# Where one layer's modulations are computed, and into how many pieces two feed-forward layers cut their hidden activations

## The reference

```python
mod = split_cols((sc @ w_mod[l] + b_mod[l])[:, None, :], (D_MODEL,) * N_MOD)
mod_x = split_cols(sc_ctx @ w_mod[l] + b_mod[l], (D_MODEL,) * N_MOD)
...
x = layer_norm(ALPHA * x + g1 * y) * ln1_g[l] + ln1_b[l]
x = layer_norm(ALPHA * x + g2 * swiglu_2(modulate(x, sh2, sc2), w_ffn_in[l], w_ffn_out[l])) \
    * ln2_g[l] + ln2_b[l]
...
def swiglu_2(h, w_in, w_out):
    a, b = h @ w_in[:, :D_FF_2], h @ w_in[:, D_FF_2:]
    return (jax.nn.silu(a) * b) @ w_out
```

## Time and profile before

| | |
|---|---|
| median of 3 runs | 3349.62 us |
| lowest and highest | 3346.73 and 3352.74 us |
| span of the profiled execution | 3342.8 us |
| PE busy | 3245.9 us, 97% of the span |
| DVE busy | 1693.8 us, 51% |
| ACT busy | 1329.2 us, 40% |
| POOL busy | 474.2 us, 14% |
| matmuls | 24670 |

### The profile page before, as it was taken

How to read it: one execution, slowest core, us unless ns; L and a number is a source line. 1 busy time by engine, 2 the same in 40 slices (tenths; PEclk the granted TensorE clock), 3 DMA queues, 4 the chain that set the end, 5 groups by cost and what they waited for, 6 DMA issues and landing times. The chain is left out here.

```text
span 3342.8 us, 59968 instructions
## 1 busy us (share of the span) xinstructions
PE 3245.9 (97%) x24670; PEld 3027.7 (91%) x24686; DVE 1693.8 (51%) x2839; ACT 1329.2 (40%) x2350; POOL 474.2 (14%) x471
## 2 busy tenths in 40 slices
PE   8999999999999999999999999999999999999998
PEld 7999988887778999999789889999998889889997
DVE  4666643546634456665545773222227646743334
ACT  4222222346633432225348663112125547552224
POOL 1010010036400010011013201001010114110100
PEclk9999999999999999999999999999999999999999
DMA  4444422122122344453201421111223212422222
GB/s 162 161 171 171 144 83 70 59 77 60 55 82 95 101 141 169 171 176 110 66 20 42 133 91 64 58 63 58 64 65 125 92 50 54 148 71 95 89 92 92
DMA packets 94973, 325.23 MB, mean 97 GB/s; under 512 B 10800, under 2 KB 15152, under 8 KB 94576
## 3 DMA queue, kind: packets, MB, share of 16 engines
q1 hardware_dynamic: 90992, 307.19, 28.0%
q0 software_dynamic: 3280, 13.68, 1.2%
q10 hardware_dynamic: 432, 0.52, 0.0%
HBM read 309.96 MB, written 2.10 MB: 93 GB/s over the span
## 5 line engine op out<-in xcount | busy, mean ns | idle before, releaser
L2403 DVE TENSOR_TENSOR r_Wbasel<-r_Wf,r_Wbaseh 128x1024 fp32r<-128x1024 f32 (+1 forms) x298 | 380.0, 1277 | 536.3 <-ACT r_Wbaseh L1770 535.9
L1770 ACT ACTIVATE r_Wbaseh<-r_Wf 128x1024 fp32r<-128x1024 f32 (+1 forms) x298 | 307.9, 1037 | 438.8 <-PE PS L1139 340.1
L1137 PE MATMUL PS<-r_X1h,r_Wbaseh 128*128 128x264 f32 (+2 forms) x1216 | 391.0, 322 | 13.0 <-DVE r_X1l L2644 3.7
L1137 PE MATMUL PS<-r_X2h,r_Wbaseh 128*128 128x256 f32 (+1 forms) x1224 | 373.4, 305 | 4.9 <-POOL r_X2l L3240 2.5
L1138 PE MATMUL PS<-r_X1l,r_Wbaseh 128*128 128x264 f32 (+2 forms) x1216 | 377.0, 310 | 0.0
L1139 PE MATMUL PS<-r_X1h,r_Wbasel 128*128 128x264 f32 (+2 forms) x1216 | 376.7, 310 | 0.0
L1139 PE MATMUL PS<-r_X2h,r_Wbasel 128*128 128x256 f32 (+1 forms) x1224 | 366.8, 300 | 0.0
L1138 PE MATMUL PS<-r_X2l,r_Wbaseh 128*128 128x256 f32 (+1 forms) x1224 | 364.1, 297 | 0.0
L2403 DVE TENSOR_TENSOR r_Wtopl<-r_Wf,r_Wtoph 128x1024 fp32r<-128x1024 f32 (+1 forms) x165 | 200.1, 1214 | 274.1 <-ACT r_Wtoph L1770 274.0
L1137 PEld LDWEIGHTS PS<-r_X1h,r_Wbaseh 128*128 128x128 f32 x1216 | 228.9, 188 | 35.7 <-issue 8.1
L1137 PE MATMUL PS<-r_X2h,r_Wtoph 128*128 128x256 f32 x872 | 248.6, 285 | 1.7 <-POOL r_X2l L3240 1.2
(11 more groups left out here) (428 smaller groups left out, 9058.3 us busy)
## 6 DMA issues: line engine op xcount, KB each, us to landing
r_Wf<-in_wmod SPq DMA_DIRECT2D x96, 512.0 KB, 3.6
r_Wf<-in_f_in SPq DMA_DIRECT2D x88, 512.0 KB, 4.4
r_Wf<-in_g_in SPq DMA_DIRECT2D x88, 512.0 KB, 3.5
r_Wf<-in_g_out SPq DMA_DIRECT2D x56, 448.0 KB, 3.3
r_Wf<-in_w_o SPq DMA_DIRECT2D x40, 512.0 KB, 4.4
r_Wf<-in_f_out SPq DMA_DIRECT2D x32, 448.0 KB, 4.2
r_Wf<-in_f_out SPq DMA_DIRECT2D x16, 512.0 KB, 4.4
r_Wf<-in_w_v SPq DMA_DIRECT2D x16, 512.0 KB, 3.5
```

The source lines that it names most:

```text
L1137: self.e.matmul(o, wh, xh, start=first, stop=False)
L1770: e.activation(p.w(i, cols)[0], p.Wf[:, i % NW, 0:cols], ACT.Copy).then_inc(*p.hi.did(i))
L2403: e.tensor_tensor(l, p.Wf[:, i % NW, 0:cols], h.bitcast(F32), ALU.subtract).then_inc(*p.lo.did(i))
```

## The change

The steps `mod_steps(1)` and the step `vectors 1` leave f2. `vectors 1` now stands behind the last output projection of the first latent layer, and the 49 steps stand in the `Group` of g0, spread over its tiles from the 13th on: with four pieces a group has 204 tile items, so one `mod` step comes every 3.67 items, where f2 had one every 2.29. Ahead of g0's group `look` is set to 1 instead of 3 (`AHEAD = 1`), and to 3 again behind it. g1 keeps 3.

g0 and g1 cut the hidden blocks into `CH4 = [(0, 5), (5, 5), (10, 6), (16, 6)]`; f1 and f2 keep `CH`. H3 has 6 blocks instead of 8, and its room takes the vectors of layer 1 (CR2) and a second JK. The bookkeeping of slots counts halves, but deals them out in the same order. The change also brings a second way of computing a feed-forward part (classes `FastFfn` and `Halves`, `fast_items`, `product`, `combine`, `sums`, `split_unit`); it is used for tags in `FAST`, and `FAST` is empty, so none of it is executed.

```diff
 CH = [(0, 8), (8, 7), (15, 7)]
+CH4 = [(0, 5), (5, 5), (10, 6), (16, 6)]
+CHS = {"f1": CH, "f2": CH, "g0": CH4, "g1": CH4}
+FAST = ()
...
-        self.H3[0], p = at("H3h", [128, 8, 768], F32R, P4)
-        self.H3[1], p = at("H3l", [128, 8, 768], F32R, p)
+        self.H3[0], p = at("H3h", [128, 6, 768], F32R, P4)
+        self.H3[1], p = at("H3l", [128, 6, 768], F32R, p)
+        CR2, p = at("CR2", [128, 2, 1024], F32, p)
+        JK2, p = at("JK2", [128, 1024], F32, p)
...
     def due(self, ready):
+        n, done = len(self.tiles) * len(self.chunks), sum(self.at.values())
+        if self.put < len(self.others) and self.put * (n - 24) < (done - 12) * len(self.others):
+            self.put += 1
+            return self.others[self.put - 1], 0, None
...
-    items.append((("vectors", 1), 0, None))
-    tiles = ffn_items(f, 4, lambda c: c, mod_steps(1))
+    tiles = ffn_items(f, 4, lambda c: c)
...
     if l == 0:
         items[-2:-2] = [(("moments", d, False), 0, None)]
-        items.append((("moments", d, True), 0, None))
+        items += [(("moments", d, True), 0, None), (("vectors", 1), 0, None)]
     tiles = []
-    for n, (j0, nj) in enumerate(CH):
+    last = len(CHS[f.tag]) - 1
+    for n, (j0, nj) in enumerate(CHS[f.tag]):
         for j in range(j0, j0 + nj):
             tiles += [(("fa", f), j, 8), (("fb", f), j, 8)]
-        if n < 2:
+        if n < last:
             tiles += [(("fo", f), (n, m), nj) for m in range(8)]
-    items.append(Group(tiles, range(nc), 5, lambda c: c))
-    items += [(("fo", f, (2, m), c), 2.4, None) for c in range(nc) for m in range(8)]
+    if f.tag not in FAST:
+        items.append((("ahead", AHEAD if l == 0 else 3), 0, None))
+        items.append(Group(tiles, range(nc), 5, lambda c: c, mod_steps(1) if l == 0 else ()))
+        items.append((("ahead", 3), 0, None))
+    else:
+        items += fast_items(f, tiles)
+    items += [(("fo", f, (last, m), c), 0.345 * CHS[f.tag][last][1], None) for c in range(nc) for m in range(8)]
...
         elif what == "vectors":
-            e.wait_ge(*p.mm.of(("mixout", 7, 1)))
+            e.wait_ge(*p.mm.of(("oo", 0, 7, 2)))
             self.vectors(*a)
```

More of the change, by code:

```diff
@@ L1051, in finished, with begin_product, end_product @@
     def finished(self, i):
-        self.fin.add(i)
+        self.fin.add(("w", i))
         self.ahead()
     def ahead(self):
[L1057 to L1063, removed]
-            self.next += 1
+        works, before = self.p.works, self.p.before
+        while self.next < len(works):
+            x = works[self.next]
+            if x[0] == "w" and x[1] > self.used + self.look:
+                return
+            if x[0] == "unit" and self.next > self.reached + self.units_ahead:
+                return
+            if any(b not in self.fin for b in before[x]):
+                return
+            if x[0] == "w":
+                self.split(x[1])
+            else:
+                self.split_unit(x)
+            self.next += 1
+    def begin_product(self, f, j, i):
+        if i == 0:
+            for n in (0, 1):
+                self.get(f.tag + "_in", (j + n * NFF,), 1024, "pair")
+        self.reached += 1
+        self.ahead()
+    def end_product(self, f, j, i):
+        self.fin.add(("unit", f.tag, j, i))
     def split(self, i):
@@ L1143, in get, with place @@
         if not raw:
[L1144 to L1147, removed]
-        return i
+            n = next(n for x, (n, h) in enumerate(self.empty) if (n, 1 - h) in self.empty[:x])
+            self.p.slot[i] = n
+            self.place(("w", i), (n, 0), (n, 1))
+        return i
+    def place(self, key, *halves):
+        self.empty = [x for x in self.empty if x not in halves]
+        found = [self.held[x] for x in halves if x in self.held]
+        self.p.before[key] = found[:1] if found[:1] == found[1:] else found
+        opened = [self.events.pop(x, []) for x in halves]
+        self.p.opened[key] = opened[0] or opened[-1]
+        for x in halves:
+            self.held[x] = key
+        if not self.p.mm.known:
+            self.p.works.append(key)
     def ahead(self):
@@ L1165, in close_slots, with product @@
     def close_slots(self, name):
         ns = self.p.slot_numbers(name)
-        self.empty = [n for n in self.empty if n not in ns]
+        self.empty = [x for x in self.empty if x[0] not in ns]
         self.closed.update(ns)
+    def product(self, f, j, i):
+        p, e = self.p, self.e
+        tag = f.tag
+        if i == 0:
+            u = [self.get(tag + "_in", (j + n * NFF,), 1024, "pair") for n in (0, 1)]
+            p.loads_of[tag, j] = u
+            p.pair_done[u[0]] = [(p.lo, ("unit", tag, j, 1)), (p.pool, ("sum", tag, j, "S4"))]
+            p.pair_done[u[1]] = [(p.lo, ("unit", tag, j, 6)), (p.pool, ("sum", tag, j, "S3"))]
+        key = ("unit", tag, j, i)
+        p.half[key] = self.empty[0]
+        self.place(key, self.empty[0])
+        weights, moving, bank, kept = PRODUCTS[i]
+        n = f.chunks[0][1]
+        if kept is None:
+            freed = {"a": ("gated", tag, j, 0), "c": ("sum1", tag, j), "b": ("sum2", tag, j)}[bank]
+            b = self.take(("product", tag, j, bank), (p.dve, freed))
+        else:
+            b = p.bank(("product", tag, j, bank))
+            e.wait_ge(*p.act.of(("kept", tag, j, kept)))
+        e.wait_ge(*p.lo.of(key))
+        if moving[0] == "T":
+            e.wait_ge(*(p.pool if moving == "T3" else p.dve).of(("combined", tag, moving)))
+        wh, wl = p.unit(key)
+        for k in range(4):
+            xh, xl = f.operand(moving, k)
+            h, l = wh[:, 128 * k:128 * k + 128], wl[:, 128 * k:128 * k + 128]
+            more = kept is not None
+            e.matmul(p.psb(b, n), h, xh, start=k == 0 and not more, stop=False, skip_group_check=more)
+            e.matmul(p.psb(b, n), h, xl, start=False, stop=False, skip_group_check=more)
+            t = e.matmul(p.psb(b, n), l, xh, start=False, stop=k == 3, skip_group_check=more)
+        t.then_inc(*p.mm.did(("product", tag, j, i), key))
+        self.empty = self.empty + [p.half[key]]
@@ L1976, in silu @@
         self.logs = False
-        e.activation(f.tm(c), p.psb(p.bank(("fa", f.tag, j, c)), f.chunks[c][1]), ACT.Silu).then_inc(
+        e.activation(f.tm(j, c), p.psb(p.bank(("fa", f.tag, j, c)), f.chunks[c][1]), ACT.Silu).then_inc(
             *p.act.did(("silu", f.tag, j, c)))
@@ new lines, in combine @@
+    def combine(self, f):
+        p, e = self.p, self.e
+        N, tag = f.norm, f.tag
+        e.wait_ge(*p.act.of(("end", N.id, 1, 7)))
+        T = [f.TR[:, t] for t in range(4)]
+        e.tensor_tensor(T[0], f.block(1, 2), f.block(1, 1), ALU.subtract).then_inc(*p.dve.did(("blocks", tag, 1)))
+        e.wait_ge(*p.dve.of(("blocks", tag, 1)))
+        e.tensor_tensor(T[1], f.block(2, 2), T[0], ALU.subtract).then_inc(*p.dve.did(("blocks", tag, 2)))
+        e.wait_ge(*p.dve.of(("blocks", tag, 2)))
+        e.tensor_tensor(T[3], f.block(2, 1), T[1], ALU.subtract).then_inc(*p.dve.did(("blocks", tag, 4)))
+        for t in (2, 1, 4):
+            e.wait_ge(*p.act.of(("blocks_high", tag, t)))
+            e.tensor_tensor(f.TL[:, t - 1], T[t - 1], f.TH[:, t - 1].bitcast(F32), ALU.subtract).then_inc(
+                *p.dve.did(("combined", tag, f"T{t}")))
@@ L3440, in weight @@
         if i >= NW:
-            if p.order[i - NW][3]:
+            if p.order[i - NW][3] == "pair":
+                for s, x in p.pair_done[i - NW]:
+                    e.wait_ge(*s.of(x))
+            elif p.order[i - NW][3]:
                 e.wait_ge(*p.dve.of(("w", i - NW)))
```

328 lines of the change are left out of this document (284 added, 44 removed).

## The result

The changed kernel takes **3357.63 us** (median of 12 runs) against 3351.68 us for the kernel before on the same chip. The ratio is **1.0023**, 95% interval 1.0014 to 1.0031: 7.7 us slower (5 to 10), where the forecast was no change and 3350 us. The time lies inside the range, 2 us from its end, and where rival A stood (3358 us).

A forecast was written before the change was run, and what follows sets the result against it. PE, busy 97% of the span, was taken as the bound. Terms -3.6 + 0.3 + 0.2 + 3.5 - 0.5 + 0.3 gave +0.2 us, a 3343.0 us span; with 6.8 us on top, 3350 us, range 3342 to 3360.

The forecast's parts named there:

- rival A: Start of g0: low look-ahead costs 8.0 us instead of 3.5, plus part of the hand-over's bound; about 3358 us, chance 0.17.
- f2 without the modulations: f2: PE's eight late starts behind DVE's low weight parts vanish; -3.6 us, other bound 0.
- Rival D: f2's pauses aren't DVE's and move to g0 with the modulation weights; 0 instead of -3.6, 3353 us; within forecast's 0.63.
- g0 with the modulations: g0's body: DVE at about half has room for the moved modulations; +0.3 us, bounds 0 and +3.6.
- Four pieces: g0 and g1: more fo tiles and additions, a split possibly in ACT's way at piece ends; +0.2 us, bounds 0 and +1.
- Start of g0: g0's start: with look 1 a wait for fa2's weight replaces the pause for the mean; +3.5 us, bounds 0 and +7.
- the case of two stretches: Start of g0: each new long pause brings its own slow clock stretch, two making the term +5.7 instead of +3.5.
- Hand-over behind g0: g0 to next layer: shorter last tiles lose cover, new step order saves squares waits; -0.5 us, bounds -4 and +5.7.
- End of g1: g1's last chain: shorter tiles bring chunk 1's end nearer to ACT's work for chunk 0; +0.3 us, bounds 0 and +2.9.
- its own sign: Start of g0: PE's waits from 1970 to 2020 us growing by more than 7 us would decide for rival A.
- B: Hand-over behind g0: the lost cover shows in full, +5.7 instead of -0.5; 3356 us, chance 0.08.

The follow-up runs named there:

- e7: Changed kernel with look 3 until the first modulation, g0 cut 5, 5, 4, 8 and g1 7, 7, 8; ratio 0.9987 to the kernel before.
- e3: Kernel before with only g0 and g1 cut 5, 5, 6, 6; modulations stay in f2, look stays 3; ratio 1.0023.
- e5: Kernel before with only g0 and g1 cut 5, 5, 5, 7; modulations stay in f2, look stays 3; ratio 0.9995.
- e1: Changed kernel, but g0 starts with look 3 and falls to 1 only ahead of the first moved modulation; ratio 1.0007 to the kernel before.
- e4: Kernel before with one edit: look 1 instead of 3 from the start of g0 to its last piece; ratio 1.0013.
- e2: Changed kernel, but the planner again assumes 2.4 instead of 2.07 for a last-piece tile of g0 and g1; ratio 1.0014 to the kernel before.
- e9: e8 with the planner assuming 2.07 for tiles of g0's last piece, giving the changed kernel's norm step order; ratio 0.9989 to the kernel before.
- e8: Changed kernel with look 3 until the first modulation, g0 cut 5, 5, 5, 7 and g1 8, 7, 7; 3342.46 us, ratio 0.9976 to the kernel before.
- e11: e8, but g0 starts with look 2 instead of 3, until the first modulation; ratio 0.9988 to the kernel before.

## Why the prediction was right or wrong

The time fell into the range, but where rival A stood, and not at the forecast: +7.8 us by the sections instead of +0.2. f2 gave 2.0 us more than its term and the two terms of +0.3 and +0.2 in g0's body came to nothing; the start of g0 cost 1.8 more than its term, the hand-over with what lies behind it 7.5 more, and the end of g1 0.8 more. That the range held is wide bounds more than insight. One reading of the text before was wrong without consequence: the measured time isn't some 7 us above the span. In every later run on record it is 1.7 to 1.9 us, so the execution whose profile stands before, with 3342.8 us, was a quick one. The forecast went from the median of the runs and isn't moved by that.

- **f2 without the modulations**: right, a little small. Predicted -3.6; the section is 4.7 us shorter in the two traces, 5.6 in the means of thirteen. I had summed eight late starts of one execution. Counted over every pair in f2 that execution has 4.3 us over the pace, and others with the modulations 4.6 to 6.6. No wait for a low part of a weight is left in f2, as forecast. Rival D falls here: no wait came up in g0's body. That the pauses belong to DVE's busy time and not to the ring places that the modulations hold isn't shown by it, since both leave f2 together; e7's one wait was the ring's.
- **g0 with the modulations**: right, and the hardest evidence is e3 beside the changed kernel: from the first to the last fo stretch both take 431.9 us, with the modulations and without. Predicted +0.3, measured 0.0. e7 shows where the cover ends.
- **Four pieces**: right by e5 (+0.2 predicted, 0.1 us measured) as to number of tiles and additions; what the cut costs comes by the last piece, below.
- **Start of g0**: the step that carried most, and its size was missed. Predicted +3.5, measured +5.3 (e1, e4). The wait for fa2 was forecast as 3.3 us and is 3.4. fa0 of chunk 1 was forecast 30.6 us behind that of chunk 0 and came 32.4 us behind it. What I left out was the `root` step of chunk 2: 2.8 us of wait, since the evacuation of its sums stands behind [both b0 1 1] in ACT's queue, and behind it a second stretch of half clock (rows by stretch, below). The waits alone give 3.4 + 2.8 - 2.2 = 4.0 us; the 1.3 that remain are about what the forecast gave for one such stretch (1.1). I had written down the case of two stretches as +5.7. That is near the 5.3, but by luck: the kernel before has one of the two already, so by the forecast's own prices the case was 3.5 + 1.1 = 4.6, and rival A's 8.0 was 6.9. The Trainium skill (TensorE: Matmul & The Clock Gate, "What's actually happening") says that the gate goes by how busy the array has been recently. The trace agrees in so far as both pauses have a stretch at 0.50 to 0.54 behind them; that every long pause has one isn't so (last section).

```profile
1985.00:1988.00 3.00, 3.00 (x14) 3.00 (x15) 2.08 (x2) 1.95 (x2) 0.00 (x0) 0.50 0.53 175
1998.00:2001.00 3.00, 3.00 (x9) 2.39 (x8) 0.64 (x2) 2.48 (x5) 1.25 (x1) 0.54 0.00 0
```

- **Hand-over behind g0**: wrong, and it decides the result. Predicted -0.5; measured +5.6 in g0 and about +1 behind it (1.4 with an added stretch of half clock; 0.9 in e1 and e3). Two errors. The order: I saw that the waits for squares would go, and they did, but I took the step moved out of their way as gone. It had only moved to stand in front of the next one, [root d0 1] (3.5 us, e2 and e9). The cover: 2.1 us of the lost 5.7 show (e2), which I had set at nothing with the argument that the order makes up for it. The 5.6 in g0 are just inside the bounds of -4 to +5.7; with the 1 us behind it the term is outside them.
- **End of g1**: predicted +0.3, measured +1.1, in every kernel with a last piece of 6 blocks (e2: +1.8, with one more stretch of half clock, from 3334 us) and in none with 7 or 8. A size, within the bounds.
- **The rivals**: A had the time (3358), but its own sign didn't come: PE's waits at the start of g0 (1965 to 2060 us) grew from 4.1 to 7.9 us, by 3.8 and not by more than 7. It priced the start of g0 at up to +8 and needed a part of the hand-over; the chip gave 5.3 and 5.6 + 1. B's +5.7 came true as well, by another mechanism for the most part. They were kept apart as exclusive cases, each with a small chance; two terms, each with more room above than below, pointed the same way, and the sum of likeliest values was lower than the likeliest sum.

## What to carry to other kernels

A step that is moved out of one waiter's way in an in-order queue stands in the next one's; walk on until the chain's last instruction, and price the whole queue, not the wait that vanishes. A look-ahead, a planner's assumed tile time or the length of the last tiles can together cost more than moving 125 us of work gains (here 5.3, 3.5 and 2.1 us against 5.6), so take them apart in runs before the bundle is judged: e8 keeps the gain and drops all three. Where several terms have wider bounds above than below, shift the sum that way.

## What the runs showed of the hardware

The half clock (granted clock 0.50) comes at places that no edit touched, in some executions and not in others. In the changed kernel's trace 38 to 44 us and 1554 to 1558 us ran at 0.72 and 0.57:

```profile
38.00:44.00 6.00, 4.69 (x27) 4.69 (x28) 3.16 (x4) 2.18 (x5) 1.68 (x3) 0.72 0.35 109
1554.00:1558.00 4.00, 3.90 (x20) 3.91 (x21) 4.00 (x6) 1.52 (x3) 0.00 (x0) 0.57 0.64 230
```

In the kernel before, at the same places of the program:

```profile
38.00:44.00 6.00, 5.05 (x41) 5.05 (x42) 2.80 (x4) 2.55 (x5) 1.51 (x2) 1.00 0.47 122
1557.00:1561.00 4.00, 3.50 (x27) 3.45 (x28) 4.00 (x5) 1.50 (x3) 0.00 (x0) 1.00 0.58 184
```

The first makes 27 starts of 41. PE had paused at both places in both executions, for 2.7 and 1.8 us, as its rows show, first the changed kernel, then the kernel before:

```profile
39.31 0.59 PE L1304 MATMUL PS<-r_X1h,r_Wtoph 128*128 128x264 f32 x1 [2.67 <-DVE r_Wtopl L2669]
1554.10 0.39 PE L1304 MATMUL PS<-r_X2h,r_Wbaseh 128*128 128x256 f32 x1 [1.83 <-DVE r_Wbasel L2669]
```

```profile
38.95 0.39 PE L1137 MATMUL PS<-r_X1h,r_Wtoph 128*128 128x264 f32 x1 [2.70 <-DVE r_Wtopl L2403]
1557.50 0.39 PE L1137 MATMUL PS<-r_X2h,r_Wbaseh 128*128 128x256 f32 x1 [1.83 <-DVE r_Wbasel L2403]
```

So the same pause brings a slow stretch in one execution and none in another. Over the thirteen profiles the section from f2's last tile to g0's first `oo` matmul, the same program in all, takes 334.1 to 334.7 us in six and 335.9 to 336.2 in seven: two levels, 1.5 us apart. The seven are those whose trace has a stretch of half clock that begins between 1554 and 1565 us. e1, e3, e4 and e11 have such a stretch near 1155 us besides, and the others none. So single profiled spans differ by some microseconds that are nobody's edit (here +2.7 of 11.4), and a sum against one trace should be made by sections that the edit touches.
